# A hybrid decoder step on one core: input stage and mixer as one program, with state and key loads, block inversion, gate rows and sample products rearranged

## The reference

```
hn   = rmsnorm(x, norm1);  proj = hn @ w_in          # xr | yr | q k v | z | gates
xc   = causal_conv(xr);    h = rglru(xc, h0)         # linear recurrence with gates from xc
out_rg  = gelu(yr) * h
q,k,v   = silu(causal_conv(qkv)); q,k normalised per head (4 heads of 128)
o, S    = gated_delta(q, k, v, g, beta, S0)          # per chunk: a triangular solve,
                                                     # decays exp(cumulated g), a state S of 128x128
out_gdn = rmsnorm(o) * silu(z)
x = x + concat(out_rg, out_gdn) @ w_out
x = x + (silu(rmsnorm(x) @ w_gate) * (rmsnorm(x) @ w_up)) @ w_down
y = rmsnorm(x, final_norm)
```

## Time and profile before

| | us |
|---|---|
| median of three runs | 1455.49 |
| the profiled execution | 1453.26 |
| its span, first to last instruction | 1451.5 |
| TensorE busy | 1377.4 (95%) |
| VectorE busy | 641.4 (44%) |
| ScalarE busy | 358.5 (25%) |
| GpSimd busy | 176.8 (12%) |
| mean granted TensorE clock | 0.964 |

### The profile page before, as it was taken

One profiled execution on the slowest core, in us unless ns is written; L12 is line 12 of the kernel. 1 busy time (PEld: TensorE's weight loads), 2 busy tenths in 40 slices (PEclk: granted clock), 3 DMA queues, 4 the chain that ended last, 5 costly groups with the idle time before them and its releaser, 6 DMA issues.

```text
span 1451.5 us, 19502 instructions
## 1 busy us (share of the span) xinstructions
PE 1377.4 (95%) x7828; PEld 1274.2 (88%) x7828; DVE 641.4 (44%) x923; ACT 358.5 (25%) x694; POOL 176.8 (12%) x238
## 2 busy tenths in 40 slices
PE   6999799998777999999999999999999999999997
PEld 5889689997775888889898989898989898989896
DVE  6446635559116455553424242424242424242426
ACT  6454533422211232232111212120202021202013
POOL 4043233240003223210000000000000000000001
PEclk9999899999856999999999999999999999999999
DMA  6111103542761444227211101010101010100003
GB/s 219 34 48 47 68 34 117 169 151 94 205 172 59 130 143 134 88 95 269 87 45 43 58 29 58 29 58 29 58 29 58 29 58 29 58 29 29 0 0 123
DMA packets 80915, 116.53 MB, mean 80 GB/s; under 512 B 18912, under 2 KB 56736, under 8 KB 80864
## 3 DMA queue, kind: packets, MB, share of 16 engines
q1 hardware_dynamic: 80864, 115.84, 23.8%
HBM read 88.04 MB, written 27.78 MB: 80 GB/s over the span
## 4 chain that ended last, share of the span: by engine, by line
PE 53%; DVE 1%; issue 0%; ACT 0%; POOLq 0%; POOL 0%; ACTq 0%
PE bank L88 17%; PE bank L87 17%; PE bank L89 17%; PE bank L2130 1%; DVE acc L2238 0%; PE bank L2131 0%; PE bank L2128 0%; DVE gu_raw L2196 0%; ACT gu_raw L2180 0%; DVE gu_first_raw L2196 0%; POOLq L2054 0%; POOL fstat L2257 0%; ACTq L2054 0%
## 5 line engine op out<-in xcount | busy, mean ns | idle before, releaser
L87 PE MATMUL bank<-ht_hi,w_hi 128*128 128x364 f32 (+1 forms) x576 | 197.3, 343 | 8.0 <-issue 8.0
L88 PE MATMUL bank<-ht_lo,w_hi 128*128 128x364 f32 (+1 forms) x576 | 190.8, 331 | 0.0
L89 PE MATMUL bank<-ht_hi,w_lo 128*128 128x364 f32 (+1 forms) x576 | 190.3, 330 | 0.0
L2208 DVE TENSOR_TENSOR hf<-sg,bank 128x364 f32<-128x364 f32 (+1 forms) x66 | 35.1, 532 | 343.6 <-PE bank L89 343.5
L87 PE MATMUL bank<-ht_hi,gu_first_hi 128*128 128x364 f32 (+1 forms) x528 | 174.1, 330 | 2.0 <-PEq L1289 2.0
L88 PE MATMUL bank<-ht_lo,gu_first_hi 128*128 128x364 f32 (+1 forms) x528 | 174.1, 330 | 0.0
L89 PE MATMUL bank<-ht_hi,gu_first_lo 128*128 128x364 f32 (+1 forms) x528 | 174.1, 330 | 0.0
L88 PE MATMUL bank<-ht_lo,gu_hi 128*128 128x364 f32 (+1 forms) x528 | 172.9, 327 | 0.0
L89 PE MATMUL bank<-ht_hi,gu_lo 128*128 128x364 f32 (+1 forms) x528 | 172.6, 327 | 0.0
L87 PE MATMUL bank<-ht_hi,gu_hi 128*128 128x364 f32 (+1 forms) x528 | 172.3, 326 | 0.0
L2238 DVE TENSOR_TENSOR acc<-acc,bank 128x512 f32<-128x512 f32 x198 | 132.7, 685 | 85.5 <-PE bank L89 85.5
(11 more groups left out here) (290 smaller groups left out, 2189.6 us busy)
## 6 DMA issues: line engine op xcount, KB each, us to landing
w_raw<-in_w_in SPq DMA_DIRECT2D x24, 512.0 KB, 4.5
dn_raw<-in_w_down SPq DMA_DIRECT2D x22, 512.0 KB, 4.3
scratch_qkv<-cb_y SPq DMA_DIRECT2D x12, 512.0 KB, 2.7
gu_first_raw<-in_w_gate SPq DMA_DIRECT2D x11, 512.0 KB, 3.6
gu_first_raw<-in_w_up SPq DMA_DIRECT2D x11, 512.0 KB, 4.4
gu_raw<-in_w_gate SPq DMA_DIRECT2D x11, 512.0 KB, 3.6
gu_raw<-in_w_up SPq DMA_DIRECT2D x11, 512.0 KB, 4.4
xin<-in_x SPq DMA_DIRECT2D x8, 512.0 KB, 4.7
```

Source lines behind the costliest of these rows:

```text
L87: pe.matmul(out, w_hi, x_hi, start=start, stop=False)
L88: pe.matmul(out, w_hi, x_lo, start=False, stop=False)
L89: return pe.matmul(out, w_lo, x_hi, start=False, stop=stop)
L2208: eng.tensor_tensor(hf[b][:, 0:m], sg[b][:, 0:m], psum[2 * b + 1][:, 0:m], ALU.mult).then_inc(hf_done, 1)
```

## The change

The two blocks become one: `input_block` and `mixer_block` return their five engine programs (`Stage`), and `build` runs the one behind the other in a single block. What the border had guarded is now waited for at single places (`st_out`, `z_out`, `wo_lo_done`, `evac_done`, `s_out`), and buffers are laid out anew: all four states have places of their own in the input stage's weight buffers, `z_in`, `v_in` and others change places, the inversion's buffers and the keys' buffers swap, `w_out` tiles 4 to 7 are loaded ahead of 0 to 3.

- SP: `z(j)` is taken apart. Order in the tail: two `w_out` tiles and weights, twice; z store; the inverses' stores; z store; two `w_out` tiles; `ts`; the compact tables; two `w_out` tiles; states 0 and 1; z store; states 2 and 3; keys and decays of chunk 1; z store; then the mixer's loads (keys 2, norm, rows, values, keys 3), the stores of the states, and only then x 0 and 1 and z.
- Gate rows are 36 ScalarE copies of one head each, in tiles j = 2 and 3 of the recurrent branch.
- Decay products: 2 behind groups 1 and 2 of tiles TQ + 1 and TQ + 2, the samples' behind group 1 of TQ + 3; GpSimd's masks in tiles 2 to 5.
- Elimination: steps 0 to 7, 8 to 13, 14 to 19 in tiles 9, 10, 11; 20 to 25 and 26 to 30 in the first two z tiles, each behind the weight split; then the samples' blocks.
- Sample products: one product of 16 columns for keys and queries together, 32 in all; queries are turned first, keys and values when their banks are evacuated.
- The states are scaled by ScalarE, 8 copies a head. VectorE's `old_part(1)` waits for the four stores of states.

```diff
@@ input_block
+    def decays_at(t, n):
+        return {(1, 1): (0, 1), (1, 2): (2, 3), (2, 1): (4, 5), (2, 2): (6, 7), (3, 1): (NC,)}.get((t, n), ())
+    def wo_tile(j, s, n):
+        return (4 * j + 2 * s + n + KT // 2) % KT
@@ SP
-            z(0, True)
+        for s in range(2):
+            load_wo(0, s)
+            load_w(TZ + s, s)
+        store_z(0, 0)
             eng.wait_ge(sol, SOL)
...
+        store_z(0, 1)
+        load_wo(1, 0)
             eng.wait_ge(d8_out, 16)
...
+        load_wo(1, 1)
             eng.wait_ge(w_hi_done, TZ + H)
             eng.wait_ge(w_lo_done, TZ + H)
             for h in range(2):
                 eng.dma_start(states[h], i["state_S"][h]).then_inc(ss_pre, 16)
-            z(1, False)
...
+        store_z(1, 0)
+        eng.wait_ge(ss_pre, 32)
+        eng.wait_ge(proj, 3 * (TZ + 3))
+        for h in (2, 3):
+            eng.dma_start(states[h], i["state_S"][h]).then_inc(ss_pre, 16)
...
+        eng.wait_ge(proj, 3 * (TZ + 3) + 1)
+        eng.dma_start(kq_all[:, :, 0:P], chunk_of(scratch["qkv"][0:2 * H], 0)).then_inc(kq_ld, 16)
+        eng.dma_start(ue_all[:, :, 0:P], scratch["ue"][0].rearrange("p (w n) -> p w n", n=P)).then_inc(kq_ld, 16)
+        store_z(1, 1)
@@ ScalarE, recurrent tile j
                 split_next(2 * j, 0, j + 2)
...
+            if j >= 2:
+                gate_rows_below(*((0, 12), (20, 32))[j - 2])
...
                     eng.activation(rb_gy[j % 2][:, a:e], bank(1, n)[:, 0:e - a], ACT.Gelu_apprx_tanh)
+                if j >= 2 and n == 1:
+                    gate_rows_below(*((12, 20), (32, MT * H))[j - 2])
+        def gate_rows_below(first, last):
+            eng.wait_ge(g_step, G_DONE)
+            for u in range(first, last):
+                c, h = u // H, u % H
+                if c < NC:
+                    ins = eng.activation(eg[:, c, h, :], tle, ACT.Copy, scale=g[:, c, h:h + 1])
+                else:
+                    ins = eng.activation(es[:, h, :], tle8, ACT.Copy, scale=g[0:TS, c, h:h + 1])
+                if h == H - 1:
+                    ins.then_inc(gr_done, 1)
@@ VectorE
-                    for j in range(0, 8):
...
+            if t >= 9:
+                for j in range(*((0, 8), (8, 14), (14, 20))[t - 9]):
+                    eliminate(xt, acomp, xtmp, BL, j, sol)
...
+                if j == 0:
+                    split_w(TZ + s + 2, s)
+                    for c in range(*((20, 26), (26, BL - 1))[s]):
+                        eliminate(xt, acomp, xtmp, BL, c, sol)
@@ GpSimd
-            for c in range(NC):
-                eng.tensor_tensor(eg[:, c, :, :], over(tle, P), spread(g[:, c, :], P, P), ALU.mult).then_inc(gr_done, 1)
-                if 1 <= t <= 4:
-                    for c in (2 * t - 2, 2 * t - 1):
+            if 2 <= t <= 5:
+                for c in (2 * t - 4, 2 * t - 3):
@@ mixer_block, TensorE
+            turn_queries(0)
+            eng.wait_ge(evac_done, TILES - 1)
                 turn_keys(0)
+            eng.wait_ge(evac_done, TILES)
                 turn_values(0)
-                turn_queries(0)
                 key_query(0)
...
-                        for q in range(2):
-                            mm = eng.matmul(out[:, q, h, b * LS:(b + 1) * LS], states[h][:, b, :],
-                                            samp_qkv[:, q * H + h, b * LS:(b + 1) * LS], start=True, stop=True)
+                    mm = eng.matmul(out[:, :, h, at], states[h][:, b, :], samp_qkv[:, h:H + h + 1:H, at],
+                                    start=True, stop=True)
@@ mixer_block, ScalarE (GpSimd's scale_states goes)
+        def scale_states(h):
+            eng.wait_ge(m_["ks_mm"], h + 1)
+            for b in range(NS):
+                ins = eng.activation(states[h][:, b, :], states[h][:, b, :], ACT.Copy, scale=esamp[:, b, h:h + 1])
+            ins.then_inc(m_["scaled"], 1)
             square_q(0)
+        scale_states(0)
             eng.activation(by_state, flat_psum(4), ACT.Copy).then_inc(m_["ks_done"], 1)
+        scale_states(1)
             square_q(1)
             copy_z(0)
+        scale_states(2)
+        scale_states(3)
```

More of the change, by code:

```diff
@@ L125, in build @@
     after_wo = B.at
[L127 to L133, removed]
+    p = Plan(nc, after_wo)
+    raw0, raw1, hi0, _, lo0 = (after_wo + 4 * D * n for n in range(5))
+    states = [Plan(nc, at)(f"s_state{h}", [P, NS, P])[:, :, :] for h, at in enumerate((raw0, raw1, hi0, lo0))]
@@ L154, in build @@
+    first = input_block(nc, i, o, scratch, psum, Plan(nc, after_wo), locals())
+    d_at = first.top
+    assert before_d <= d_at
+    p = Plan(nc, d_at)
+    gu_first_raw = p("gu_first_raw", [P, 2, KT, P])
+    at = p.at
+    mix_buf["vp"], mix_buf["mp"], mix_buf["d0"], kt1 = (p(name, [P, H, P]) for name in ("vp", "mp", "d0", "kt1"))
     gu_first_hi = Plan(nc, at)("gu_first_hi", [P, 2, KT, P], F32R)
-    at = B.at
-    mix_buf["kt"] = [B(f"kt{s}", [P, H, P]) for s in range(2)]
-    mix_buf["rhs"], mix_buf["z"] = B("rhs", [P, H, P]), B("z", [P, H, P])
+    at = p.at
@@ new lines, in build, with _ @@
+    with nc.Block() as block:
+        @block.sync
+        def _(eng):
+            first.sync(eng)
+            second.sync(eng)
+        @block.tensor
+        def _(eng):
+            first.tensor(eng)
+            second.tensor(eng)
+        @block.scalar
+        def _(eng):
+            first.scalar(eng)
+            second.scalar(eng)
+        @block.vector
+        def _(eng):
+            first.vector(eng)
+            second.vector(eng)
+        @block.gpsimd
+        def _(eng):
+            first.gpsimd(eng)
+            second.gpsimd(eng)
@@ new lines, in tensor @@
+        last = MT - 1
+        turn_o(last)
+        project(last, rg_steps)
+        turn_x(last - 1)
+        project(last, o_steps)
+        eng.wait_ge(gu_first_done, 2)
+        eng.wait_ge(m_["mq_done"], MT)
+        eng.wait_ge(m_["x23_done"], 2 * NC)
+        m = GROUPS[0][1]
+        for q in range(2):
+            for f in range(KT):
+                mm = mm3(eng, psum[2 + q][:, 0:m], gu_first_hi[:, q, f, :], gu_first_lo[:, q, f, :],
+                         ht_hi[:, f, 0:m], ht_lo[:, f, 0:m], f == 0, f == KT - 1)
+            mm.then_inc(k["gu_mm"], 1)
@@ L2000, in ffn_block @@
+    return Stage(sync, tensor, scalar, vector, gpsimd, None, None)
 def ffn_block(nc, i, o, scratch, psum, B, k):
```

2782 lines of the change are left out of this document (1376 added, 1406 removed).

## The result

The changed kernel takes 1405.15 us (median of four runs, 1404.62 to 1406.63) where the kernel before took 1454.86 beside it: a ratio of 0.966, 95% interval 0.9645 to 0.9678. It is 49.7 us faster; the forecast was 1404. The profiled execution has a span of 1403.1 us (before 1451.5).

What follows compares the result with a forecast made beforehand. TensorE was taken as the bound nearly everywhere, idle in a few stalls, each followed by low clock. 5.6 + 9.4 + 16.0 + 13.6 + 6.0 = 50.6 us off 1453.3 gave 1402.7 (1404.9 against the median); forecast 1404, 8-in-10 range 1391 to 1417.

Steps and rivals of the forecast that it cites:

- Gate rows: Input stage: gate rows moved from GpSimd to ScalarE remove the 4.2 us stall and 1.4 us of low clock; gain 5.6.
- Decay products: Input stage: spreading them over three tiles removes a 7.1 us stall and 2.6 us of low clock; gain 9.4 after 0.4 wait.
- The border: Between input stage and mixer: last evacuation at 392.9 instead of 403.6, sample products at 394.9 instead of 410.9; gain 16.0 us.
- the 9.8 us of the projections: Late projections end at 380.2 instead of 390.0; not a term by itself, because ScalarE's last evacuation is late next.
- Sample products: Mixer's sample part: half the passes, with 16 columns, bound by weight loads; 13.7 us instead of 27.3, gain 13.6.
- Rival (e): Sample products: passes with two strided pieces of 8 columns cost as much as two passes; 13.6 less gain, 1418; chance 0.03.
- Scaling: Sample stage: ScalarE scales the states instead of GpSimd, unhindering VectorE's output norm; gain 4.8 plus 1.2 of low clock, 6.0.
- The 1.2 us for the low clock: Sample stage behind the norm's stall: at most 1.2 of the 4.4 us lost to low clock counted as gain.
- Rival (a): Border: the last output weights come late, restart at 400 instead of 393, gain 8 smaller; 1412 us; chance 0.18.
- Rival (b): Sample products mostly at 2.4 GHz take 7 instead of 13.7 us, and 4.4 us behind the norm go; 1394; chance 0.12.
- (c): Projections 1 to 3: ScalarE becomes the late one and the decay stall keeps 3 to 6 us; 1409 us; chance 0.08.
- (d): Mixer loop stays at the lower clock; a 22.0 us tile loses up to 22, all eight give 1580; chance 0.02.

Runs made afterwards that it cites:

- u_rows: Changed kernel with the gate rows built again by GpSimd in eight three-tensor steps instead of ScalarE's 36 copies; 1414.20 us, ratio 0.9740 to the kernel before.
- u_elim: Changed kernel with the elimination again in three tiles (8, 10 and 13 steps) instead of five; 1409.61 us, ratio 0.9691 to the kernel before.
- i_evac: Changed kernel with the last tile's evacuation moved on ScalarE ahead of the copy of the last two output weights; 1407.20 us, ratio 0.9678 to the kernel before.
- c_fill: Changed kernel with eleven unread 128x512 products added on TensorE behind the turned queries to fill the 9.6 us wait; 1407.91 us, ratio 0.9677.
- i_early: i_evac plus loads of the first two states and third pair of output weights ahead of the wait for the inverse; 1406.00 us, ratio 0.9660.
- u_products: Changed kernel with the sample products again as 128 passes of 8 columns instead of 64 of 16; 1418.95 us, ratio 0.9775 to the kernel before.
- i_both: Changed kernel with the edits of i_loads and i_norm together; 1394.77 us, ratio 0.9596 to the kernel before.
- i_norm: Changed kernel with the sample rows' output norm moved on VectorE behind the third state update; 1405.58 us, ratio 0.9663 to the kernel before.
- r_changed: The changed kernel run again without edits, on another chip, giving its second profile; 1408.61 us, ratio 0.9682 to the kernel before.
- i_loads: i_early plus states 2 and 3 loaded ahead of the tables, and first values ahead of chunk 2's keys; 1394.67 us, ratio 0.9602.

## Why the forecast was right, step by step

**Gate rows, 5.6:** 6.05 by u_rows. The summed savings of VectorE's steps and the 1.4 us of low clock were the right way to read it. **Decay products, 9.4:** 9.6. The table changes cost what the earlier trace rows said: a load of 1.28 us, and the exponential starts 1.30 us behind the load's start. It happens in two more tiles than before, and all of it is hidden (ScalarE's timeline of the changed kernel, tile 2):

```profile
176.00 1.28 ACT L829 ACT_TABLE_LOAD   x1
177.30 1.08 ACT L829 ACTIVATE eg<-bank 128x512 f32<-128x512 f32 x2
```

The Trainium skill (ScalarE: Activation LUTs, "What ACT_TABLE_LOAD costs") gives 2.66 us for a change of set, load plus drain. The measurement decides: the load's 1.28 us is in the trace, but the exponential follows it at once, no drain was paid there, and TensorE waits for no exponential.

**The border, 16.0:** 16.3, and the stations were right too: compact store 13.8 us earlier than the earlier trace rows (15.0 said, and the start was 1.4 late), last evacuation 25.8 (25.7 said), a wait of 9.6 (about 10 said). The sentence that the 9.8 us of the projections are no term by themselves is what u_elim shows. One reason was incomplete. I read the late weights as a matter of what stands ahead of them on SP; it is that, but the 16 DMA engines themselves are busy at 0.96 from 355 to 398, which the earlier trace rows couldn't show (0.60 and 0.25 in the stretches I had asked for). I had estimated 1.3 us a transfer and the values at 410, "wanted at 412"; in the trace they were issued at 390.83 and 0.7 late, 1.8 late in the second profile, and 1.9 to 4.3 in i_evac, c_fill, u_elim and i_early.

**Sample products, 13.6:** 13.1 to the solve, the half microsecond being that wait. Rival (e) is out: 0.216 us for 16 columns (13.84 / 64), 0.215 for 8 (27.48 / 128 in u_products). **Scaling, 6.0:** this step is mis-sized. 4.8 came from "unhindered such an instruction takes 0.67"; but the norm stayed at 1.75 us, because GpSimd's next block of the turned table (1.26 us, at 413.61) moved up beside it. Four traces bear this out: the norm takes 5.48 us beside 3.77 us of GpSimd scaling, 1.75 beside the whole 1.26 us of this block, 1.24 where it overlaps only its end (i_both, 404.50 against 403.92) and 0.68 behind it (i_norm). That leaves 3.7. The 1.2 us for the low clock didn't come: it returned for the last state products, at 410.92 and 416.75. Even the 3.4 us of the whole stretch hang on the clock's course: in r_changed the stretch takes 27.6 us, 2.3 more than in the kernel before.

The errors: +1.0 upstream, +0.3, -0.5, -2.6, +0.9 behind M5 and -1.4 ahead of M1 sum to -2.3 (48.4 against 50.6 with rounding), less than two profiles of the same kernel differ by (1403.1 and 1411.1). So the mechanisms of the terms are right and one is mis-sized, while a sum as near as 2 us is in part luck: the second profile, 8 us longer, would have put it 10 off. One reading was wrong without consequence: TensorE starts the feed-forward block at 664.17 in the kernel before, so what stays behind the mixer is 787 us, not 782.

Of what was to show it, all points but one came: no gate or decay wait, 0.6 us in the late projections, a wait of 9.6 us ahead of the values' turn, 64 products in 13.84 us. The one that failed is "no instruction of VectorE over 2 us in the sample stage": the norm is at 1.75, but the second of the expansions `kq_all<-z,cs` still takes 2.28 us, beside GpSimd's block of 1.86 us at 400.81 (VectorE's timeline of the changed kernel). The prediction had said itself that GpSimd's inverse start still hinders the expansions; the pair took 3.42 us before as well.

```profile
401.46 2.28 DVE L1860 TENSOR_TENSOR kq_all<-z,cs 64x1024 f32<-64x1024 f32 x1
```

Rival (a) didn't happen. Rival (b), the clock back sooner, didn't either: all 64 products ran at 0.50. Its 6.7 us for them is more than any run showed (2.3 in c_fill, 4.2 in i_loads, where the clock fell among the products without a wait ahead of them), and what was won there went into waits for the next loads. (c) and (d) are out: no wait of TensorE for ScalarE in projections 1 to 3, loop tiles of 22.0.

## What to carry to other kernels

- Where several stalls stand in a row, undo them one by one in thought: a stall ahead of a wait for something else (9.6 us of projections here) is worth nothing until that something moves.
- Look at the share of the DMA engines in the very stretch between the last dense work and the restart. Here it was 0.92 to 0.99, and moving one or two loads made others late (waits of 8.1, 8.5 and 4.3 us); what helped was to give the queue the order in which TensorE wants the data, all of it at once.
- When a GpSimd instruction beside a VectorE one is taken away, ask which GpSimd instruction moves up into its place.

## What the runs showed of the hardware

- The same kernel on the same data has more than one course of TensorE's clock: the sample stage took 21.9 us in one profile and 27.6 in another, with clock 0.71 and 0.50. In c_fill and i_loads the clock fell from 1.00 to 0.50 among the sample products though TensorE had not stood ahead of them. What decides between the courses is open.
- A pass with 128 columns of weights and 16 of data takes 0.216 us at 1.2 GHz (13.84 / 64 at clock 0.50), and one with 8 of data as much. At 2.4 GHz (clock 1.00) the first 21 took 2.52 in c_fill, 0.12 each.
- Transfers in short pieces hold the DMA engines: in i_early 98 GB/s at a share of 0.91 from 365 to 375 (the tables; 7783 of 7788 packets under 512 bytes), against 327 GB/s at 0.88 in the ten us before. The share isn't a hard mark: the view gives 1.23 for the same ten us in i_both.
- A VectorE instruction with a GpSimd one beside it takes longer: the norm 0.68 us alone, 1.75 beside 1.26 us, 5.48 beside 3.77 us of GpSimd; a convolution step 1.38 alone and 2.04 beside the earlier trace rows.
